# Twenty-eight up matrices per layer read as a quarter and three quarters, and routing products of 108 columns, in a two-layer mixture-of-experts trunk

## What is computed

```python
def hier_moe(x, w_group, w_expert, w_gate, w_up, w_down):
    xf = x.reshape(n, d)
    group_logits = (xf @ w_group).astype(jnp.float32)
    ...
    expert_logits = (xf @ w_expert).astype(jnp.float32).reshape(n, N_GROUPS, EXPERTS_PER_GROUP)
    ...
    for e in range(N_EXPERTS):
        hid = jax.nn.silu(xf @ w_gate[e]) * (xf @ w_up[e])
        out = out + combine[:, e:e + 1] * (hid @ w_down[e]).astype(jnp.float32)
```

## Time and profile before

| What | Value |
|---|---|
| three runs | 1305.0, 1307.29, 1307.72 us; median 1307.29 us |
| the profiled execution | 1307.29 us, of which span 1305.5 us |
| TensorE busy | 1045.1 us (80%) |
| VectorE, ScalarE, GpSimd busy | 483.5, 176.1, 108.7 us |
| read from DRAM | 472.08 MB |
| the chain that ended last | PE 47%, DMA 46% |

### The profile page before, as it was taken

How to read it: one execution, slowest core, us unless ns; L and a number is a source line. 1 busy time by engine, 2 the same in 40 slices (tenths; PEclk the granted TensorE clock), 3 DMA queues, 4 the chain that set the end, 5 groups by cost and what they waited for, 6 DMA issues and landing times.

```text
span 1305.5 us, 26625 instructions
## 1 busy us (share of the span) xinstructions
PE 1045.1 (80%) x11057; PEld 641.9 (49%) x11057; DVE 483.5 (37%) x965; ACT 176.1 (13%) x413; POOL 108.7 (8%) x233
## 2 busy tenths in 40 slices
PE   9999989666766676679999999999675676756778
PEld 7885555333433333344688884555333333333333
DVE  2987534111111111136685888524121111211127
ACT  2343211000000000011111110211010000000011
POOL 0010111000010000000110110011000000000000
PEclk9999899888888888889999999998888888888889
DMA  9866999999999999999454237899999999999992
GB/s 362 303 268 266 358 426 424 428 431 426 429 430 427 429 430 426 430 411 387 146 188 159 102 133 313 333 426 426 427 428 429 428 428 429 429 427 430 428 419 100
DMA packets 59266, 473.87 MB, mean 363 GB/s; under 512 B 4328, under 2 KB 6632, under 8 KB 34000
## 3 DMA queue, kind: packets, MB, share of 16 engines
q1 hardware_dynamic: 57952, 469.73, 87.2%
q10 hardware_dynamic: 912, 2.12, 0.4%
q0 software_dynamic: 352, 1.32, 0.3%
HBM read 472.08 MB, written 3.16 MB: 364 GB/s over the span
## 4 chain that ended last, share of the span: by engine, by line
PE 47%; DMA 46%; issue 2%; DVE 2%; SPq 1%; ACT 0%; POOL 0%; DVEq 0%; POOLq 0%; ACTq 0%
DMA big<-in_moe_w_up_dram 43%; PE ps L1048 10%; PE ps L769 6%; PE ps L1267 6%; PE ps L1287 4%; PE ps L845 3%; PE ps L744 3%; PE ps L1179 3%; DMA big<-in_moe_w_down_dram 2%; PE ps L1073 2%; PE ps L725 1%; DMA big<-in_ple_w_gate_dram 1%; PE ps L735 1%; PE ps L1014 1%; PE ps L1081 1%
## 5 line engine op out<-in xcount | busy, mean ns | idle before, releaser
L1048 PE MATMUL ps<-big 128*32 128x256 f32 x4048 | 323.6, 487 | 236.5 <-DMA big<-in_moe_w_up_dram 232.6
L1048 PEld LDWEIGHTS ps<-big 128*32 128x32 f32 x4048 | 167.3, 139 | 391.3 <-issue 230.2
L1997 DVE SCALAR_TENSOR_TENSOR wroute<-wroute,ps 64x256 f32<-64x256 f32 x64 | 26.4, 413 | 649.2 <-ACT wroute L1521 649.2
L1073 PE MATMUL ps<-big,r 128*32 128x256 f32 x2048 | 122.8, 379 | 2.4 <-DVE r L2006 2.1
L1521 ACT ACTIVATE wroute<-ps 64x256 f32<-64x256 f32 x64 | 24.2, 378 | 546.8 <-PE ps L1048 546.8
L2509 POOL TENSOR_TENSOR big<-big,rk 128x64 f32<-128x64 f32 x64 | 28.4, 444 | 733.7 <-PE ps L1060 711.9
L1073 PEld LDWEIGHTS ps<-big,r 128*32 128x32 f32 x2048 | 64.5, 110 | 37.7 <-DVE r L2006 3.8
L1081 PE MATMUL ps<-big 32*128 32x256 f32 x1024 | 73.3, 400 | 1.3 <-ACT big L1532 1.3
L1014 PE MATMUL ps<-xn,big 128*32 128x256 f32 x1024 | 67.3, 380 | 1.6 <-POOL big L2503 1.6
L1081 PEld LDWEIGHTS ps<-big 32*128 32x128 f32 x1024 | 46.3, 184 | 29.1 <-issue 27.7
L1371 ACT ACTIVATE big<-ps 128x256 f32<-128x256 f32 (+3 forms) x58 | 25.5, 454 | 173.6 <-PE ps L1267 48.5
(11 more groups left out here) (296 smaller groups left out, 1202.0 us busy)
## 6 DMA issues: line engine op xcount, KB each, us to landing
big<-in_moe_w_gate_dram SPq DMA_DIRECT2D x62, 2048.0 KB, 32.9
big<-in_moe_w_down_dram SPq DMA_DIRECT2D x61, 2048.0 KB, 38.5
big<-in_moe_w_up_dram SPq DMA_DIRECT2D x60, 2048.0 KB, 37.1
big<-in_od_w_in_dram SPq DMA_DIRECT2D x12, 2048.0 KB, 14.1
big<-in_ev_w_in_dram SPq DMA_DIRECT2D x5, 2048.0 KB, 21.3
big<-in_ple_w_gate_dram SPq DMA_DIRECT2D x8, 1024.0 KB, 19.8
big<-in_od_w_out_dram SPq DMA_DIRECT2D x4, 2048.0 KB, 7.8
big<-in_ev_w_out_dram SPq DMA_DIRECT2D x2, 2048.0 KB, 14.0
```

The lines of the kernel that those rows point to most:

```text
L1048: ins = nc.tensor.matmul(ps[TOK * i:TOK * i + TOK, 5, 0:2 * P].rearrange("p (b n) -> p b n", b=2), xe[:, k, :], here, start=k == 0, stop=k ...
L1073: ins = nc.tensor.matmul(ps[TOK * q:TOK * q + TOK, 7, 0:QD], hidT[:, k, :], wd[:, k, q * QD:(q + 1) * QD], start=k == 0, stop=k == KF - 1)
```

## The change

For experts 4 to 31 the up matrix is read in two transfers. `expert_up_low` takes rows 0 and 1 (4 KB of each partition's 16 KB) into the expert's own up place, `expert_up_high` rows 2 to 7 (12 KB) into the place before it, (e - 1) modulo 3. The high part of expert 4 thus goes into the rows of place 0 that stood empty, after expert 0's read and not after expert 1's, and those of experts 5 and 6 also move one expert ahead. From expert 7 on both parts are issued behind the same wait as the whole matrix was. The high part's landing counts on the semaphore of the gate matrix that is issued next to it, so PE waits for twice the count there. Expert 31's up matrix comes in four transfers instead of three.

The routing product moves 108 columns instead of 36: three neighbouring k blocks of `wroute`, placed in the bank so that the wanted block always falls on columns 72 to 107 (`LOGITS`). The other columns hold sums that nobody reads. VectorE reads its 36 columns at 72 instead of 0.

```diff
+ROUTE = NG + NE
+WIDE = 3
+LOGITS = (WIDE - 1) * ROUTE
+LOW = 2
...
     twice = kind == GATE and ring_turn(GATE, EARLY) == j
-    return l * (sum(ring_turn(kind, e) == j for e in range(NE) if e != apart) + twice)
+    high = kind == GATE and sum(ring_turn(GATE, e) == j for e in range(EARLY, LAST))
+    return l * (sum(ring_turn(kind, e) == j for e in range(NE) if e != apart) + twice + high)
...
+            def expert_up_low(l, e, j):
+                sync.dma_start(held(EXPERT_SLOTS[l][j][UP], KD, BLK)[:, 0:LOW, :].unsqueeze(1),
+                               eu[l][:, ds(e, 1), 0:LOW, :]).then_inc(weights_landed[j][UP], 16)
+            def expert_up_high(l, e, j):
+                sync.dma_start(held(EXPERT_SLOTS[l][(j - 1) % DEPTH][UP], KD, BLK)[:, LOW:KD, :].unsqueeze(1),
+                               eu[l][:, ds(e, 1), LOW:KD, :]).then_inc(weights_landed[(j - 1) % DEPTH][GATE], 16)
...
                 sync.dma_start(place[:, HALF:KD, :], eg[l][:, EARLY, HALF:KD, :]).then_inc(begun, 16)
+                expert_up_high(l, EARLY, EARLY % DEPTH)
                 expert_read(l, DOWN, 0)
                 expert(l, DOWN, DEPTH, 0)
                 for e in range(EARLY, EARLY + DEPTH):
                     expert_read(l, UP, e - DEPTH)
-                    expert(l, UP, e, e % DEPTH)
+                    expert_up_low(l, e, e % DEPTH)
                     if e < EARLY + DEPTH - 1:
                         expert(l, GATE, e + 1, e % DEPTH)
+                        expert_up_high(l, e + 1, (e + 1) % DEPTH)
...
                         holder[EXPERT_SLOTS[l][ring_turn(kind, e)][kind]] = expert_read, l, kind, e
+                        if kind == UP and e > NE - DEPTH:
+                            holder[EXPERT_SLOTS[l][(e - 1) % DEPTH][UP]] = expert_read, l, UP, e
...
                     for k in range(KD):
-                        ins = nc.tensor.matmul(b[:, 0:NG + NE], xT[:, k, t * P:(t + 1) * P], wroute[:, l, k, :],
-                                               start=k == 0, stop=k == KD - 1)
+                        first = min(WIDE * (k // WIDE), KD - WIDE)
+                        at = LOGITS - (k - first) * ROUTE
+                        ins = nc.tensor.matmul(b[:, at:at + WIDE * ROUTE].rearrange("p (a n) -> p a n", a=WIDE),
+                                               xT[:, k, t * P:(t + 1) * P], wroute[:, l, first:first + WIDE, :],
+                                               start=k == 0, stop=k == KD - 1, skip_group_check=True)
```

More of the change, by code:

```diff
@@ L581, in last_parts @@
                     ks = slice(bounds[i], bounds[i + 1])
+                    if kind == UP:
+                        if i == 0:
+                            sync.dma_start(dst[:, 0:LOW, :], eu[l][:, LAST, 0:LOW, :]).then_inc(landing, 16)
+                            ks = slice(LOW, bounds[1])
+                        high = held(EXPERT_SLOTS[l][(LAST - 1) % DEPTH][UP], KD, BLK)
+                        sync.dma_start(high[:, ks, :], eu[l][:, LAST, ks, :]).then_inc(landing, 16)
+                        continue
                     sync.dma_start(dst[:, ks, :], (eg, eu, ed)[kind][l][:, LAST, ks, :]).then_inc(landing, 16)
@@ L679, in _ @@
                         e = it * DEPTH + EARLY + j
-                        for kind in (UP, DOWN):
-                            expert_read(l, kind, it * DEPTH + EARLY - DEPTH + j)
-                            expert(l, kind, e, (EARLY + j) % DEPTH)
+                        expert_read(l, UP, it * DEPTH + EARLY - DEPTH + j)
+                        expert_up_low(l, e, (EARLY + j) % DEPTH)
+                        expert_up_high(l, e, (EARLY + j) % DEPTH)
+                        expert_read(l, DOWN, it * DEPTH + EARLY - DEPTH + j)
+                        expert(l, DOWN, e, (EARLY + j) % DEPTH)
                         expert_read(l, GATE, it * DEPTH + EARLY - DEPTH + 1 + j)
@@ L1027, in weights @@
                         j = ring_turn(kind, e)
+                    if kind == GATE and (e is None or e >= EARLY):
+                        n = n * 2 - (e == LAST)
                     if kind == GATE and j == ring_turn(GATE, EARLY) and e != j:
@@ L1038, in gate_up @@
                     high = w
+                    if e is None or e == LAST:
+                        rows = held(EXPERT_SLOTS[l][(j - 1) % DEPTH][UP], KD, BLK).rearrange("p k (b h n) -> p k h b n", b=2, h=2)
+                        high = [rows[:, LOW:HALF], rows[:, HALF:KD]]
                     if e == LENT[1]:
@@ L1043, in gate_up @@
                         if e == LAST and k in (0, *LAST_PARTS[0]):
-                            pe.wait_ge(part_landed[0][sum(b <= k for b in LAST_PARTS[0])], 16 * (l + 1))
+                            pe.wait_ge(part_landed[0][sum(b <= k for b in LAST_PARTS[0])], (16 + 16 * (k == 0)) * (l + 1))
                         for i in range(4):
-                            up = (w[1][:, k] if high is w or k < 2 else high[0][:, k - 2] if k < HALF else high[1][:, k - HALF])
+                            up = (w[1][:, k] if high is w or k < LOW else high[0][:, k - LOW] if k < HALF else high[1][:, k - HALF])
                             here = w[0][:, k, i % 2] if i < 2 else up[:, i % 2]
@@ L1914, in moe @@
                     full(dve, f"route{l}_{t}")
-                    emptied(f"route{l}_{t}", ve.tensor_scalar(lg[:, t, :], bank(f"route{l}_{t}")[:, 0:NG + NE],
+                    emptied(f"route{l}_{t}", ve.tensor_scalar(lg[:, t, :], bank(f"route{l}_{t}")[:, LOGITS:LOGITS + ROUTE],
                                                               nrm[:, 2 + t:3 + t], None, ALU.mult))
```

## The result

| Kernel | Median, us | Runs, lowest to highest | Ratio to before, 95% interval |
|---|---|---|---|
| before, beside it | 1306.01 | 21 runs, 1304.97 to 1309.39 | 1 |
| changed | 1309.49 | 21 runs, 1307.82 to 1311.17 | 1.0020 [1.0014, 1.0026] |
| changed, once more on another occasion | 1309.06 | 12 runs, 1308.15 to 1310.65 | 1.0012 [1.0003, 1.0022] |

By the ratios the changed kernel is slower by 0.20% on the first occasion and by 0.12% on the other, 2.6 and 1.6 us; the medians lie 3.5 and 1.8 us apart. Its own time hardly moved between the two; that of the kernel before was 1306.01 us on the first and 1307.3 on each of three later ones. On the first occasion twelve runs of before stand at 1305.0 to 1306.1 us and nine at 1306.9 to 1309.4, and the median falls into the lower group; the means, 1306.5 there and 1307.2 to 1307.4 later, moved less. The forecast was 1308.8 us and +0.12%.

What follows compares the result with a forecast made beforehand. Bound inside the expert plateaus: bytes over the DMA rate, from when the engines are continuously busy. 1307.29 + 4.3 (split) - 2.8 (clock) + 0 = 1308.8 us, +0.12%; range for 8 in 10, 1304.2 to 1312.2 us.

Steps and rivals of the forecast that it cites:

- The split transfer, +4.3 us: In both layers' expert plateaus, 56 up transfers of 2 MB get 128 more pieces each, at 0.076 us per split transfer.
- nothing or 8.5 us: Split cost in the plateaus: nothing if pieces are free (chance 0.17), 8.5 us if 12 KB pieces count as two (0.07).
- half a megabyte at a time: Rival: low parts of expert up matrices move at 320 GB/s, 23 us more, 1327.5 us; chance 0.02.
- the 112 us: Split cost by the skill's fixed 2.0 us per transfer, 56 in line; the prediction held that the rows disagree.
- The earlier reads, 0: Expert 4's high part issued earlier in a full queue ends nothing sooner; rival that they do more, chance 0.08.
- The wide products' own cost, 0: In routing, 108 columns hide under the 113 ns per PE instruction; 0.7 us of layer 0 kept for the range.
- the 136 ns of the straight line: Routing product of 108 columns, on a line between 36 and 192 columns: 0.7 us more per layer.
- The clock, -2.8 us: Layer 0 routing: wide products keep the clock up, shrinking the DMA hole by 2.8 us; rival that it falls anyway, 0.16.
- the chance of slower by over 0.2%: Chance that the changed kernel measures above 1309.9 us: 0.35.
- 0 in layer 1: Wide products gain nothing at layer 1's routing, since its transfer queue is full there.
- PE, SP and the waits for slots have slack there: Inside the expert plateaus only DMA sets the time; SP stood 485.1 us waiting for slots.

Runs made afterwards that it cites:

- kernel with two pieces: Kernel before with wide products, up matrices of experts 4 to 30 each in one transfer with halves exchanged, two 8 KB pieces per partition: 1309.55 us, 1.0014.
- split in place: Kernel before with wide products, up matrices of experts 4 to 30 in 4 KB and 12 KB transfers, no earlier reads: 1310.53 us, 1.0024.
- run with every second partition: Kernel before with wide products, up matrices of experts 4 to 30 in two transfers of 64 alternate partitions, 16 KB each: 1305.84 us, 0.9987.
- two runs with doubled products: Each token tile's routing products made twice: 36 columns on the kernel before, 1320.18 us; 108 columns on it with wide products, 1309.49 us.
- split alone: Changed kernel with routing products back at 36 columns, keeping split transfers and earlier reads: 1313.11 us, 1.0037 of the kernel before.

## Why the prediction came out nearly right

**The split transfer, +4.3 us.** Right. The changed kernel and the wide products alone were not run on one occasion; by their ratios to the kernel before, the split costs 1.0020 - 0.9986 and 1.0012 - 0.9986 of 1307 us, 4.4 and 3.4 us. The kernel with two pieces, beside the wide products alone, paid 3.9 us where 54 x 0.076 = 4.1 was due. The links of the step held: the plateau at 426 to 427 GB/s, and the price per piece and not per transfer. The rate alone gives (428 - 426.5) / 428 of the two plateaus' 860 us, 3 us, and 4 us at 426. The split in place, 4.8 us above the wide products, leaves some 1 us for anything else, and the 0.6 us of the run with every second partition isn't told from nothing. Neither bound, nothing or 8.5 us, came near, and half a megabyte at a time isn't slow in a full queue. Three readings in the prediction were loose. Two of the 56 matrices, expert 31's, came in parts already; the packets rise from 59266 to 67330, by 56 x 128 pieces and 896 small ones, so the price is not touched. The 1327.5 us for slow half megabytes left out the 4.3 us, and the earlier trace rows shows engines that are 0.89 busy, not a nearly empty queue. And the 2.0 us of the Trainium skill, DMA: Bandwidth & Descriptors, from which the 112 us came, are given in its section on the anatomy of one DMA for transfers that GpSimd issues; those here are SP's.

**The earlier reads, 0.** Not contradicted. The hole of layer 0 is as small without them (1.5 us of transfer time missing from 150 to 158 us with the wide products alone, by 291 and 406 GB/s, against 1.9 in the changed kernel), and the split in place stands within 1.6 us of the whole change. Nothing was found that the earlier reads do; a gain of some 1.5 us is not excluded.

**The wide products' own cost, 0.** Right: 3.79 us for 32 instructions in both kernels. Neither the 136 ns of the straight line nor any addition showed; the 108 columns hide under the 113 ns, whatever sets these.

**The clock, -2.8 us.** The mechanism was right: the clock stays, the routing is through in 10.42 us, the hole shrinks by 2.3 us, SP goes on 2.9 us earlier, and in the two runs with doubled products the fall goes with the columns. The sum for one execution also came out, +1.66 us where +1.5 stood, but that was partly luck: the other profiled execution of the changed kernel is 2.93 us above that of before. What failed is the size of this term. It was read from one profiled execution in which the clock fell in layer 0 and not in layer 1, and entered in full. Between medians the wide products gave 1.6 and 2.1 us. Two things take from the 2.8. Even against the execution with the fall, layer 0's weights landed only 2.0 and 2.3 us earlier. And the kernel before has executions down to 1304 us, as low as with wide products, so likely not every one has the fall. The mean granted clocks on record speak for it: of the 71 runs of before beside the experiments, 24 have 0.911 or more and a median of 1306.0 us, 47 have 0.910 or less and 1307.9 us; with wide products alone all 22 have 0.912 or more, and 1305.5 us. A mean over an execution does not say where the clock fell, so this share, about two in three, is inferred. The text had seen that ("this does not happen every time") and didn't put it into the sum. With 3.9 - 1.6 or 3.9 - 2.1 it would have been +1.8 to +2.3 us, and the chance of slower by over 0.2% should have been nearer to a half than to a third.

**"0 in layer 1".** Wrong as a rule, harmless for the execution it was read from. "Its queue is full there" was read from an execution without a fall. In the split alone the clock fell in layer 1 too, the first products came 13.2 us behind the routing (835.88 to 849.10) and the queue ran short by 1.6 us. In the changed kernel the wide products also buy off that fall: the split with 36 columns is 3.3 to 4.05 us slower than with 108, although the wide products gain only about half as much on the kernel before.

**A place that the prediction did not have.** "PE, SP and the waits for slots have slack there" does not hold for PE at the end of layer 0 in every execution. In three profiled executions (the second of the changed kernel, the split in place, the two pieces) expert 31's products in layer 0 ran at a reduced clock, in 4.9 to 5.4 us instead of 3.7, and they end the layer in place of the last landing; in the changed kernel that is 1.1 us. In before and the wide products alone those of expert 30 were slow instead, 6.5 us, and the landing covered them. So a part of the 3.9 and 4.8 us of these two kernels may be this and not the pieces; one profile each doesn't say how often it comes.

**What stays open.** Why the fall should come in layer 1 more readily with the split reads than without is not shown: the products there are the same, and only what PE did before them is shifted. Nor is it shown how often each execution has a fall, and where: unprofiled runs have only a mean clock. And the kernel before's own median moved between 1306.01 and 1307.3 us from one occasion to the next, which is the difference between +0.20 and +0.12%; the two groups of its runs were met in other shares, and no run here tells why.

The version to keep is the kernel before with the wide products alone, at 0.9987 [0.9979, 0.9996] and 0.9985 [0.9975, 0.9995].

## What to carry to other kernels

Where transfers run without a gap, price a change of their shape by pieces: compare the rate in windows with pieces of other sizes, and multiply the difference by the number of pieces; starting bytes earlier in a queue that is already full gave nothing back here that could be told from zero. A gain that comes from a fall of the clock seen in one profile should enter the sum with the share of executions that have it, as far as their mean clocks tell, and with what reaches the end of the path. Before calling a place covered, look for the same place in an execution in which its cause is present.

## What was not expected of the hardware

- Two transfers of 64 neighbouring partitions each, in place of one of 128, brought the rate from 428 down to 225 GB/s with all DMA engines busy; two of every second partition cost nothing (428 GB/s).
- The clock fell to 1.2 GHz while PE and its weight loads were busy for 4.00 of 4 us, on products of 36 columns, and stayed at 2.4 GHz on products of 108 columns whose PE instructions took 114 ns each at that clock.
- A further piece in a transfer costs about 9 ns on its DMA engine between 16 KB and 8 KB as between 16 KB and 2 KB, and a further transfer in a full queue nothing that could be measured.
- In two executions of the changed kernel the 64 PE instructions of expert 31's gate and up took 3.66 us at a granted clock of 1.00 and 5.35 us at 0.64, behind 2.70 and 2.94 us in which PE waited for the same transfer.
